# Three gaps of 64 bytes in the SBUF layout of a two-block transformer kernel: where the rows used as matmul weights begin

## What is computed

```python
def reference(x, mem, ...):
    x = first_block(x, mem, ...)     # 2 layers: attention + memory attention, gated, added to x
    return second_block(x, ...)      # 2 layers: three attentions, then 16 experts, top 2 of a group

# the products that carry the work
proj = jnp.einsum('bsd,de->bse', h, w_in)            # 1024 -> 11264, 3584, 1892, 1892 columns
x    = x + jnp.einsum('bse,ed->bsd', y, w_out[i])    # 1536 or 1024 -> 1024
h = silu(einsum('nd,edf->enf', xt, w_gate)) * einsum('nd,edf->enf', xt, w_up)
y = einsum('enf,efd->nd', h, w_down)
```

## Time and profile before

| | |
|---|---|
| median of 3 runs | 1149.97 us (1147.03 to 1153.93) |
| profiled execution, its own time | 1149.28 us |
| its span | 1147.9 us |
| PE busy | 1105.9 us (96%) |
| weight loads (PEld) busy | 917.1 us (80%) |
| DVE busy | 890.2 us (78%) |
| ACT busy | 746.9 us (65%) |
| granted TensorE clock, mean | 0.989 |

### The profile page before, as it was taken

The page is one execution under the profiler, slowest core; times in us unless marked ns, Lnnn a source line. Parts: engine busy times, 40 slices in busy tenths (PEclk is TensorE's granted clock), DMA queues, the critical chain, the costliest instruction groups (busy, mean ns, idle before and its releaser), DMA issues.

```text
span 1147.9 us, 14686 instructions
## 1 busy us (share of the span) xinstructions
PE 1105.9 (96%) x5515; PEld 917.1 (80%) x5515; DVE 890.2 (78%) x1476; ACT 746.9 (65%) x1325; POOL 0.2 (0%) x4
## 2 busy tenths in 40 slices
PE   7999999999999999999999999999999999999996
PEld 5788888888787888888977787877778878787774
DVE  4756757777768867766578769999977886999996
ACT  5746665655666665577465557888855655688883
POOL 0000000000000000000000000000000000000000
PEclk9999999999999999999999899999999999999998
DMA  8654454443433455534452416999927332599991
GB/s 291 231 198 147 147 184 148 158 171 111 149 145 111 171 195 181 197 110 153 153 173 74 147 38 201 353 361 367 369 88 243 111 112 72 167 361 356 370 356 41
DMA packets 131844, 221.26 MB, mean 193 GB/s; under 512 B 6145, under 2 KB 77361, under 8 KB 131761
## 3 DMA queue, kind: packets, MB, share of 16 engines
q1 hardware_dynamic: 127920, 213.21, 54.4%
q10 hardware_dynamic: 3840, 6.98, 1.8%
HBM read 219.13 MB, written 1.05 MB: 192 GB/s over the span
## 4 chain that ended last, share of the span: by engine, by line
PE 78%; DVE 11%; ACT 6%; issue 2%; DMA 2%; ACTq 0%; DVEq 0%
PE bank L488 21%; PE bank L490 20%; PE bank L489 20%; PE bank L851 4%; PE bank L787 3%; DVE wL L441 2%; PE bank L637 1%; ACT wH L433 1%; DMA ring<-in_w_mem_kv 1%; PE bank L836 1%; PE bank L2274 1%; PE bank L2323 1%; ACT S L810 1%; PE bank L1735 1%; PE bank L2288 1%
## 5 line engine op out<-in xcount | busy, mean ns | idle before, releaser
L441 DVE TENSOR_TENSOR wL<-ring,wH 128x1024 fp32r<-128x1024 f32 (+1 forms) x316 | 375.3, 1212 | 127.4 <-ACT wH L433 126.2
L433 ACT ACTIVATE wH<-ring 128x1024 fp32r<-128x1024 f32 (+1 forms) x316 | 320.3, 1047 | 31.5 <-PE bank L490 14.1
L488 PE MATMUL bank<-wH,hTH 128*128 128x512 f32 (+2 forms) x592 | 235.7, 398 | 3.3 <-DVE wL L441 2.3
L490 PE MATMUL bank<-wH,hTL 128*128 128x512 f32 (+2 forms) x592 | 229.8, 388 | 0.0
L489 PE MATMUL bank<-wL,hTH 128*128 128x512 f32 (+2 forms) x592 | 229.3, 387 | 0.0
L488 PEld LDWEIGHTS bank<-wH,hTH 128*128 128x128 f32 x592 | 111.7, 189 | 25.9 <-DVE wL L441 4.5
L490 PEld LDWEIGHTS bank<-wH,hTL 128*128 128x128 f32 x592 | 111.5, 188 | 21.9
L489 PEld LDWEIGHTS bank<-wL,hTH 128*128 128x128 f32 x592 | 111.8, 189 | 20.2 <-issue 0.5
L488 PE MATMUL bank<-wH,xgH 128*128 128x512 f32 x256 | 104.5, 408 | 0.0
L490 PE MATMUL bank<-wH,xgL 128*128 128x512 f32 x256 | 100.4, 392 | 0.0
L489 PE MATMUL bank<-wL,xgH 128*128 128x512 f32 x256 | 100.0, 391 | 0.0
(11 more groups left out here) (296 smaller groups left out, 1866.2 us busy)
## 6 DMA issues: line engine op xcount, KB each, us to landing
ring<-in_w_in_a SPq DMA_DIRECT2D x44, 1024.0 KB, 5.1
ring<-in_w_out SPq DMA_DIRECT2D x20, 1024.0 KB, 4.9
ring<-in_w_down SPq DMA_DIRECT2D x20, 1024.0 KB, 7.2
ring<-in_w_gate SPq DMA_DIRECT2D x36, 512.0 KB, 5.4
ring<-in_w_up SPq DMA_DIRECT2D x36, 512.0 KB, 7.1
ring<-in_w_in_b SPq DMA_DIRECT2D x14, 1024.0 KB, 5.2
ring<-in_w_mem_kv SPq DMA_DIRECT2D x8, 1024.0 KB, 7.1
ring<-in_w_in SPq DMA_DIRECT2D x8, 1024.0 KB, 5.4
```

The source lines that it names most:

```text
L433: act.e.activation(quarter_parts(q)[0], quarter_in_ring(q), COPY).then_inc(w_high, 1)
L441: dve.e.tensor_tensor(lo, quarter_in_ring(q), hi.bitcast(F32), SUB).then_inc(w_low, 1)
L488: pe.e.matmul(o, a[0], b[0], start=first, stop=False)
L490: return pe.e.matmul(o, a[1], b[0], start=False, stop=last)
```

## The change

Three lines move the running address on by 64 bytes:

```diff
     X = sb("X", P, 2, D)
+    top_of[0] += 64
     hT = [sb(f"hT{n}", P, 8, TOK, dt=F32R) for n in "HL"]
 ...
     kT = sb("kT", P, 4, TOK)
+    top_of[0] += 64
     S = sb("S", P, 2, 4, TOK)
     PT = sb("PT", P, 2, 2, 4, P)
     Y = sb("Y", P, 2, 1536)
+    top_of[0] += 64
     G = sb("G", P, 2, 1536)
     arena = sb("arena", P, 2 * 1892)
```

## The result

The changed kernel takes 1160.49 us (median of 6 runs, 1156.71 to 1163.44), the kernel before 1149.51 us (6 runs, 1147.03 to 1153.93). The ratio is 1.0093, with a 95% interval of 1.0063 to 1.0122: slower by about 11 us, where 32.5 us (1182 us) were forecast. The profiled span went from 1147.9 to 1158.6 us.

A forecast was written before the change was run, and what follows sets the result against it. PE was taken as the bound. Misaligned loads add 47.1 us, less 3.6 hidden in experts, 8 at stops and 3 in tails: +32.5 us on 1149.28, so 1182 us, range 1168 to 1196.

The forecast's parts named there:

- PE as the bound, and no other engine touched: Whole kernel: PE, busy 1105.9 of 1147.9 us, sets the time; address changes cost ACT and DVE nothing.
- I take 13.3 ns: Weight loads of L488 to L490, `xs` and `OHT`: each misaligned load costs PE 13.3 ns; 3536 loads, +47.1 us.
- What costs: PE matmuls: the loaded row's misalignment by 512 costs 32 cycles (13.3 ns) per load; misaligned streams were taken as 0.
- What is hidden: PE's extra time is partly absorbed where it waits anyway: 3.6 us in experts, 8 at stops, 3 in tails.
- Stops: Outside the experts, PE's waits for ACT or DVE absorb extra time: some 35 stops at 0.24 us, 8 us.
- Experts: In the experts DVE is nearly full, so each expert grows 0.36 us instead of 0.48; 3.6 us hidden over some 30.
- Tails: After a stop PE already runs slower for a while, and this may not add: 3 us for some 60 tails.
- Edits costed at nothing: Float32 matmuls, transposes, cuts by ACT and DVE, and newly misaligned streams: 0 us each.
- A finer unit: Only some offsets pay: 1174 us if 128 is free, 1155 to 1160 if 64 is free; chance 0.12.
- Nothing hidden: No extra PE time is absorbed and misaligned streams add 2 us: 1198 us; shares chance 0.77 with the likeliest case.
- No price: Offset is free; the slow tiles share a place above 128,000 in the partition instead: 1148 to 1149 us; chance 0.07.
- Faster: Aligned load and stream collide by starting at the same place of 512; offsets separate them: 1129 us; chance 0.04.

The follow-up runs named there:

- e3: Kernel before with all turned (loaded) rows and the streaming quarters `wH`, `wL` at 64: 1147.56 us, ratio 0.999.
- e7: Kernel before with `hT` at 192, `yTH` and `yTL1` at 256, `xg` at 384, `mhT` and `gh` at 448, streams at 0: 1151.86 us in one run.
- e9: Kernel before with `hT`, `yTH` and `yTL1` at 32, `xg` at 192, `mhT` and `gh` at 256: 1157.95 us in one run.
- e12: Kernel before with everything from `X` on shifted by 256, load and stream equal by 256: 1147.65 us, ratio 0.9979.
- e8: Kernel before with `hT` at 128, `yTH` and `yTL1` at 448, `xg` at 32, `mhT` and `gh` at 0: 1157.93 us in one run.
- e2: Kernel before with only the low halves `hTL`, `xgL`, and `mhT`, `gh` at 64; high halves and `yTL1` at 0: 1156.25 us in one run.
- e11: Kernel before with only the layers' rows `hT`, `yTH`, `yTL1` at 64; `S`, `xg`, `mhT`, `gh` at 0: 1157.43 us, ratio 1.0059.
- e1: Kernel before with all turned (loaded) rows behind `X` at 320, streams at 0: 1162.67 us, ratio 1.0128.
- e13: Kernel before with `hT` at 96, `yTH` and `yTL1` at 160, `xg`, `mhT` and `gh` at 224: 1163.26 us in one run.
- e6: Kernel before with only the streaming quarters `wH` and `wL` moved to 64, loaded rows left in place: 1152.04 us, ratio 1.0023.
- e10: Kernel before with only the high halves `hTH` and `xgH` at 64, all the rest at 0: 1158.6 us in one run.
- e5: Kernel before with `T0` and all behind it moved by 192 bytes, so `yT2L` and `yTL0` are aligned too: 1146.96 us, ratio 0.9993.

## Why the prediction was wrong, step by step

**The price of a triple** (mean in ns over settled triples; 680 is no price), by the address of the load less that of the stream, when all three loads have the same difference:

| difference, by 256 | ns | seen at |
|---|---|---|
| 0 | 680 to 684; `gh` behind a paying `xg` 684.2 to 686.4 | before; load and stream both at 64 (e3); 256 (e7, e9, e12) |
| 32 | 699.5, 700.0 | e8, e9 |
| 64 | 699.8 to 700.2 | after, e2, e11; 320 in e1 |
| 96 | 702.8 | e13 |
| 128 | 697.7, 698.0, 698.1 | after, e8; 384 in e7 |
| 160 | 700.5 | e13 |
| 192 | 686.7 to 689.6 | after, e7, e9; 448 in e7, e8; -64 in e6 |
| 224 | 699.9 | e13 |

The streams were at 0 or at 64 only (e3, e6), so that "load less stream" rests on two places of the stream.

- **PE as the bound, and no other engine touched: right.** PE's busy time took up 10.1 of the 10.7 us, and the busy times of DVE and ACT stayed within 1.0 us.
- **"I take 13.3 ns" for each of 3536 loads, +47.1 us: this step failed.** 13.3 ns was rightly read, for one load of three (e2 has 13 at 64 too). But I multiplied it by three for triples in which all three are off. Those cost 20 ns and not 40 (e1, at the offset of the earlier trace rows itself), and two cost 19 (e10). The rows had no triple with more than one load off, so that adding was an assumption that I did not name. A row with all loads off would have been needed, or a bound: 13.3 to 40 ns per triple. The lower end would have given 1200 x 13.3 ns = 16 us gross. The prediction said that its mechanism is wrong if the pace on `hT` is not 240 ns a matmul; it is 233.3.
- **What costs: half right.** I put it on the loaded side alone ("it is the loaded side that pays"). e3 and e6 show that load and stream count together, by 256. Under that rule `gh` and `mhT` at 192 cost 8 to 10 ns and not 40, and `xs` and `OHT`, for which the sum had 128 x 13.3 ns = 1.7 us, cost 0.1 us together where the clock is full: the rows that stream against them moved with them, save the `ys` of one group. The argument that a rule in units of 256 that spares 64 would have spared 320 did hold: 64 costs what 320 costs.
- **The sum with the right prices.** 592 triples on `hT` x 19.0 ns, 256 on `xg` x 13.5, 128 on `gh` x 7.9, 64 on `yTL1` x 19.6, 64 on `mhT` x 9.6, and 0.5 us for `yTL0` and `yT2L`, each by its means before and after: 11.2 + 3.5 + 1.0 + 1.3 + 0.6 + 0.5 = 18 us gross, where 11 were measured.
- **What is hidden: 14.6 us forecast, some 6 measured.** PE's 5515 matmuls stand in both traces in the same order, so that the distances from start to start can be subtracted one from the other. Where the clock is full in both, they grew by 11.9 us, of 18 us that are priced; 1.7 us went back in the low stretches, which lie elsewhere in the two executions.
  - *Stops (8 us)*: net nothing, idle time went from 42.0 to 42.6 us.
  - *Experts (3.6 us)*: some 2.4 are hidden. The prices of 128 triples on `xg` and 64 on `gh` are 2.2 us a pass, and at full clock a pass grew by 1.0 to 1.1; in e1, with 3.8 us of prices, it grew by 1.8.
  - *Tails (3 us)*: this one is real. Of 478 triples on `hT` that have another triple behind them, 371 are settled, and 371 x 19.0 ns = 7.0 us is nearly all that the 478 grew by (335.3 to 342.4 us). So those just after a stop or other work paid next to nothing. With the 50 that have other work behind them 2.7 us were not paid.
  - *The rest*, which the forecast did not have: 64 triples on `hT` stream fewer than 512 columns and paid 0.1 us where 1.2 are priced, `mhT` and the `yT` tiles paid 1.1 less than priced, PE's other work took 0.3 less, and against it all stands the wait for `X`, 1.6 us longer.
- **Edits costed at nothing: right.** The float32 matmuls and the cuts of ACT and DVE kept their durations. So did the idle matmuls, in which one element streams again and again: 218 ns from start to start with `identR` at 384 and at 64.
- **The rivals.** *A finer unit* (0.12): its number, 1155 to 1160, comes near the result, but not its mechanism, since 64 pays in full and only 192 is cheap. *Nothing hidden* (1198) fell with the price. *No price* (0.07) fell with e1 and e12: the same tiles pay at 320 and don't at 256, and where they lie in the partition does not matter. The Trainium skill ("TensorE: Matmul & The Clock Gate", "Step-by-step: what each phase is for") gives PE two independent read ports of SBUF. If that is taken to mean that addresses can't matter, the runs disagree: 686.7 ns instead of 680 when the stream alone moves by 64 bytes (e6). *Faster* (0.04): its seed, that load and stream meet by their addresses, was right with the sign turned round. The aligned pair is the best of those tried.

**Not settled.** Why 192 is cheap, and what the loads and streams share, no run shows. Nor do triples with mixed differences follow from the table. Written as the differences of the three loads, 192, 192, 0 took 691.9 ns on `yTL0` and 697.5 on `yT2L` in e6, and 697.6 on `yT2L` in e7: more than three times 192, 686.7. And 64, 64, 128 took 693.2 to 693.4 (`yTL0` and `yT2L` in e1, `yT2L` in e2), 128, 128, 64 took 688.2 (`yT2L` in e8): less than three times 64 or three times 128. These are 14 to 18 triples each. So with three loads off the price can be 8 or 13 ns as well as 20, and "saturates" holds only for loads with the same difference. The step from one load's place to the next may have a price of its own; that was not tried.

No version beats the kernel before: e3, e5 and e12 are at its time, with 1 inside their intervals.

## What to carry to other kernels

Where fp32r matmuls of 512 columns run back to back with a new weight load each, let the weight rows and the streaming rows begin at the same place by 256 bytes; here three loads off by the same difference cost 6.7 ns together at 192 and 18 to 23 ns at all others tried, 1 to 3% of the pace, and 0.9% of the kernel. A common shift of both sides is free, so align them to each other before spending padding on 512. And when a price has been read from a mix in which one part of three pays, don't multiply it up: keep the case that it doesn't add as one end of the range.

## What was not expected of the hardware

- The address of the *stream* changes the pace by itself: 64 bytes more on `wH` and `wL` turn 680.0 into 686.7 ns (e6), and the same 64 bytes on both sides give 680 again (e3).
- With one difference for all loads that are off, the price saturates: 13, 19 and 20 ns for one, two and three loads at 64 (e2, e10, after); at 320, 13.3 and 20 for one and three (before, e1).
- It is not even in the difference: 32, 64, 160 and 224 cost 20 ns, 128 costs 18, 96 costs 23, 192 costs 6.7, which is 16 cycles of 2.4 GHz where 20 ns are 48.
- Not all matmuls show it. fp32r triples of 512 columns pay in full. Those on `hT` with 452 and 416 columns, of which every second one streams from off 256 in the kernel before as well, went from 612.3 to 619.7 ns and from 567.2 to 567.4. The float32 matmuls of 256 columns stay at 216 ns from start to start when the difference goes from 0 to 128 (`qT2` with `kT`), those on `PT` at 112 ns from 0 to 64.
